# Fills that stay on one product before the level stage, four logarithms in one place, and an earlier split of the mLSTM read-out

## The reference, cut to what matters

```python
xn = _rms_norm(x, P['norm_mix_pre'][l])
cols = jnp.einsum('btd,dc->btc', xn, P['w_in'][l])
ca, cb, cc, cg = _split(cols, [A_COLS, B_COLS, C_COLS, N_BRANCH * D_MODEL])
h_a = mLSTM(ca)                 # mixer A, its read-out: sigmoid(o) * h
h_b = window_attention(cb)      # mixer B
h_c = rwkv(cc)                  # mixer C
gates = jax.nn.sigmoid(cg).reshape(Bsz, T, N_BRANCH, D_MODEL)
merged = (gates[:, :, 0] * (h_a @ P['w_branch_a'][l])
          + gates[:, :, 1] * (h_b @ P['w_branch_b'][l])
          + gates[:, :, 2] * (h_c @ P['w_branch_c'][l]))
mix = merged @ P['w_out'][l]
```

```python
mean = jnp.mean(y, axis=-1, keepdims=True)
var = jnp.mean(jnp.square(y - mean), axis=-1, keepdims=True)
y = ((y - mean) * lax.rsqrt(var + GN_EPS)).reshape(Bsz, T, C_W) * gn_g + gn_b
```

## Time and profile before

| | |
|---|---|
| median of 3 runs | 2463.97 us (2463.54 to 2465.94) |
| the profiled execution: its time, its span | 2466.26 us, 2464.5 us |
| PE busy | 2336.3 us, 95% |
| DVE, ACT, POOL busy | 997.6, 901.3, 786.4 us |
| ACT_TABLE_LOAD | 69 of 1283 ns |
| mean granted TensorE clock | 0.976 |

### The profile page before, as it was taken

How to read it: one execution, slowest core, us unless ns; L and a number is a source line. 1 busy time by engine, 2 the same in 40 slices (tenths; PEclk the granted TensorE clock), 3 DMA queues, 4 the chain that set the end, 5 groups by cost and what they waited for, 6 DMA issues and landing times.

```text
span 2464.5 us, 53615 instructions
## 1 busy us (share of the span) xinstructions
PE 2336.3 (95%) x23450; PEld 2225.3 (90%) x23450; DVE 997.6 (40%) x1559; ACT 901.3 (37%) x1751; POOL 786.4 (32%) x630
## 2 busy tenths in 40 slices
PE   7999989999899899999989999999998989999997
PEld 7998888888789899999989988888887989999997
DVE  4426654455434522320073276545444534332102
ACT  4345532213354522222344455223323444233222
POOL 3332222112235244444324222222112433444441
PEclk9999989999999999999999999999999999999998
DMA  5532211111214132322334221111112242233331
GB/s 162 135 88 65 61 36 32 28 49 32 60 50 143 57 91 86 90 86 86 82 107 130 61 74 48 28 49 32 28 41 63 72 131 61 87 92 89 89 86 52
DMA packets 334193, 180.82 MB, mean 73 GB/s; under 512 B 33528, under 2 KB 330648, under 8 KB 332936
## 3 DMA queue, kind: packets, MB, share of 16 engines
q1 hardware_dynamic: 333776, 177.34, 26.0%
q10 hardware_dynamic: 184, 0.05, 0.0%
HBM read 167.98 MB, written 9.38 MB: 72 GB/s over the span
## 4 chain that ended last, share of the span: by engine, by line
PE 81%; DVE 10%; ACT 4%; issue 3%; DMA 1%; POOL 1%; SPq 0%; DVEq 0%; ACTq 0%; POOLq 0%
PE psum_products L657 72%; PE psum_mixer L657 7%; DMA w_raw<-in_w_in 1%; ACT w_high L1221 1%; DVE xn_low L2047 1%; DVE merged L2041 1%; DVE x L1671 1%; ACT L1221 0%; ACT c_in_rate L1221 0%; DVE squares_ffn L1665 0%; DVE gate_product L2039 0%; POOL w_low L2270 0%; DVE squares L1638 0%; PE psum_mixer L1036 0%; SPq L2118 0%
## 5 line engine op out<-in xcount | busy, mean ns | idle before, releaser
L2270 POOL TENSOR_TENSOR w_low<-w_raw,w_high 128x512 fp32r<-128x512 f32 (+2 forms) x606 | 761.5, 1278 | 1562.4 <-ACT w_high L1221 1561.0
L657 PE MATMUL psum_products<-xn_high,w_high 128*128 128x272 f32 (+1 forms) x3424 | 741.3, 298 | 43.0 <-POOL w_low L2270 14.2
L657 PE MATMUL psum_products<-xn_high,w_low 128*128 128x272 f32 (+1 forms) x3424 | 713.2, 290 | 0.0
L657 PE MATMUL psum_products<-xn_low,w_high 128*128 128x272 f32 (+1 forms) x3424 | 712.1, 290 | 0.0
L657 PEld LDWEIGHTS psum_products<-xn_high,w_high 128*128 128x128 f32 x3424 | 545.1, 190 | 64.2 <-issue 32.8
L657 PEld LDWEIGHTS psum_products<-xn_low,w_high 128*128 128x128 f32 x3424 | 546.1, 191 | 0.0
L657 PEld LDWEIGHTS psum_products<-xn_high,w_low 128*128 128x128 f32 x3424 | 542.8, 191 | 0.0
L1221 ACT ACTIVATE w_high<-w_raw 128x512 fp32r<-128x512 f32 (+2 forms) x606 | 331.2, 595 | 169.8 <-PE psum_products L657 140.1
L657 PE MATMUL psum_products<-hidden_high,w_high 128*128 128x272 f32 x704 | 145.9, 288 | 0.0
L657 PE MATMUL psum_products<-hidden_high,w_low 128*128 128x272 f32 x704 | 145.7, 288 | 0.0
L657 PE MATMUL psum_products<-hidden_low,w_high 128*128 128x272 f32 x704 | 145.1, 288 | 0.0
(11 more groups left out here) (373 smaller groups left out, 2991.7 us busy)
## 6 DMA issues: line engine op xcount, KB each, us to landing
w_raw<-in_w_in SPq DMA_DIRECT2D x112, 512.0 KB, 4.0
w_raw<-in_w_ffn_in SPq DMA_DIRECT2D x88, 512.0 KB, 3.8
w_raw<-in_w_ffn_out SPq DMA_DIRECT2D x32, 512.0 KB, 3.9
w_raw<-in_w_out SPq DMA_DIRECT2D x16, 512.0 KB, 3.9
w_raw<-in_w_ffn_out SPq DMA_DIRECT2D x16, 384.0 KB, 3.3
x_kept<-x SPq DMA_DIRECT2D x2, 2176.0 KB, 7.6
x<-x_kept SPq DMA_DIRECT2D x2, 2176.0 KB, 9.0
w_raw<-in_w_in SPq DMA_DIRECT2D x16, 256.0 KB, 3.8
```

Of the source, the lines that this page charges most:

```text
L657: return pe.matmul(out, lhsT, rhs, start=start, stop=stop, skip_group_check=True)
L2270: low_ready.inc(pool.tensor_tensor(wl[:, n % NSPLIT, ks_], wraw[:, slot, ks_], wh[:, n % NSPLIT, ks_].bitcast(F32), ALU.subtract))
```

## The change

It has three parts. First, `fill` gets a second argument. In `c_prep`, `c_keys` and `c_scale` (which is `c_keys` on PE) it is False, and the fill then takes steps of the next unit alone. In the other steps it takes two units as before. Second, `c_variance` on ACT copies the variance out of PSUM (scale 1/64) instead of taking its logarithm, and `c_rsqrt` takes all logarithms (two instructions of 1090 columns) and then two Exps of the same size. DVE waits for the second Exp before block 2. Third, `a_out_split` moves from behind the last unit of `cols_c` to the place ahead of `b_out(8)`.

```diff
@@ WEIGHT @@
+          ... "a_out_split": 0.0 ...
@@ make_plan @@
             second += [("b_scores", l, c + 2)] if c < 7 else []
+            second += [("a_out_split", l)] if c == 7 else []
...
-        plan += [("a_out_split", l), ("gate", l) + GATES[0], ("c_shift_out", l)]
+        plan += [("gate", l) + GATES[0], ("c_shift_out", l)]
@@ tensor engine @@
-            def fill(steps):
+            def fill(steps, on=True):
...
-                while steps > 0 and u < len(units) and u < unit_at[0] + 2 and fillable(units[u]):
+                while steps > 0 and u < len(units) and u < unit_at[0] + 1 + on and fillable(units[u]):
...
-                fill(2)
+                fill(2, False)
...
-                fill(4)
+                fill(4, False)
...
             def c_keys(l, g):
-                fill(8)
+                fill(8, False)
@@ scalar engine @@
-                    step(fn(y_rn[:, f, c0:c1], mp[2 + b][:, 0:c1 - c0], ACT.Ln, scale=1.0 / 64, bias=C("scalars", 1, 1)),
-                         bank[2 + b].empty["act"])
+                    step(fn(y_rn[:, f, c0:c1], mp[2 + b][:, 0:c1 - c0], ACT.Copy, scale=1.0 / 64), bank[2 + b].empty["act"])
 
             def c_rsqrt(l):
-                step(fn(y_rn[:], y_rn[:], ACT.Exp, scale=-0.5), flow("c_gn_r"))
+                for f in (0, 2):
+                    step(fn(y_rn[:, f:f + 2, :], y_rn[:, f:f + 2, :], ACT.Ln, bias=C("scalars", 1, 1)))
+                for f in (0, 2):
+                    step(fn(y_rn[:, f:f + 2, :], y_rn[:, f:f + 2, :], ACT.Exp, scale=-0.5), flow("c_gn_r"))
@@ vector engine @@
-                if f == 0:
+                if f % 2 == 0:
                     flow("c_gn_r").wait_next(dve, "dve")
```

More of the change, by code:

```diff
@@ L165 @@
 WEIGHT = {"c_prep": 1.0, "c_keys": 1.0, "c_scaled": 0.3, "c_scale": 1.0, "c_gram": 0.7, "c_level": 0.3, "c_chain": 0.5,
-          "c_state_out": 0.0, "a_chunk": 0.6, "a_chunk_out": 0.5, "a_state_out": 0.0, "a_state_put": 0.0, "b_put": 0.0, "c_shift_put": 0.0, "c_state_put": 0.0, "a_scale": 0.3, "a_out": 0.2, "b_values": 0.5,
+          "c_state_out": 0.0, "a_chunk": 0.6, "a_chunk_out": 0.5, "a_out_split": 0.0, "a_state_out": 0.0, "a_state_put": 0.0, "b_put": 0.0, "c_shift_put": 0.0, "c_state_put": 0.0, "a_scale": 0.3, "a_out": 0.2, "b_values": 0.5,
           "b_scores": 0.6, "b_out": 0.6}
```

## The result

| | before | changed |
|---|---|---|
| median of 5 runs | 2463.54 us | 2450.94 us |
| lowest to highest | 2461.34 to 2465.94 | 2442.94 to 2457.63 |
| ratio, with its 95% interval | 1 | 0.9948 [0.9924, 0.9971] |
| profiled execution | 2466.26 us | 2442.94 us |

The change makes the kernel 12.6 us faster, where 18.6 us were forecast. The direction and the range hold, and so does the forecast's own range of 2439 to 2452 us, but the median lies 5.5 us above the predicted 2445.4 us. The changed kernel's runs spread over 14.7 us. A second set of runs in the experiments has a trace of a usual execution.

What follows compares the result with a forecast made beforehand. PE was taken to bound the kernel, busy 2336.3 of 2464.5 us. Per layer 5.9 + 3.4 + 0 = 9.3 us, 18.6 us for both, gave a median of 2445.4 us, range 2436 to 2460 us (forecast's own 2439 to 2452).

Steps and rivals of the forecast that it cites:

- The logarithms: Variance stage: 4.2 us of PE's idle time and 1.7 us of low clock won, 5.9 us per layer.
- The cover: Behind c_rsqrt: DVE's 2.59 us wait for PE and 3.0 us before branch C hide a 2.3 us later start.
- The fills: Groups of mixer C: ACT's and DVE's chain starts sooner, PE owes steps; 3.4 us per layer won.
- I leave that out: Steps PE owes go into levels, chains and variance, some filling a level that had none; this was not counted.
- the owed steps: Fill steps PE hasn't done by a group's first c_kprime product; in group 4 four steps, 2.9 us.
- The split: Read-out split at the attention's end: new 3.7 us wait against c_prep's clock; taken as 0, from -3.7 to +3 per layer.
- The prediction's sign against this term: The prediction is wrong in the read-out split if the clock stays at 0.5 in c_prep.
- A: Slower: PE waits for DVE in order at b_out and each c_scaled; 2471.6 us, chance 0.08.
- B: Only the squares' waits go, clock falls as often, fills win nothing; 8.4 us, 2455.6 us, chance 0.18.
- C: No change: PE's total work is the same and the waits only move; 2464 us, chance 0.08.
- D: More: POOL wait goes in full, clock stays high in c_prep and after; 16 us per layer, 2432 us, chance 0.08.

Runs made afterwards that it cites:

- logarithms alone: Kernel before, with only the variance blocks' logarithms gathered in c_rsqrt: 2451.23 us, ratio 0.9952.
- fills alone: Kernel before, with only the fills of c_prep, c_keys and c_scale kept on the next unit: 2451.39 us, ratio 0.9946.
- split alone: Kernel before, with only the read-out split moved ahead of b_out(8): 2467.74 us, ratio 1.0008.
- fills and logarithms: Kernel before, with the fill and logarithm edits together and the read-out split where it was: 2444.09 us, ratio 0.9917.
- changed, first trace: The whole change against the kernel before, first set of runs: median 2450.94 us, ratio 0.9948; its trace is the fastest execution, 2442.94 us.
- changed, once more: The whole change, unaltered, measured again against the kernel before: 2451.39 us, ratio 0.9945; trace of a usual execution, span 2451.0 us.
- split one step later: Changed kernel with the read-out split directly behind b_out(8), ahead of the last cols_c unit: 2436.88 us, ratio 0.9896 to the kernel before.
- c_prep only: Kernel before with the logarithm edit and only c_prep's fills kept on the next unit, split not moved: 2445.17 us, ratio 0.9921.

## Why the prediction was right or wrong

The stages of layer 0, each the difference of two starts in PE's timeline. The marks are the last probabilities' transposes, `c_tanh_w`'s product (mixer C begins), the first `c_kprime` product of groups 0 and 4, the first and the last squares' product, and branch C's first matmul:

```
                        transposes  mixer C   group 0   group 4    first      last        sum
                        -> mixer C  -> grp 0  -> grp 4  -> first   -> last    -> branch C
                                                        squares    squares
before                    16.86     22.07    296.69     33.96      26.07      32.54      428.19
logarithms alone          16.87     22.09    296.78     33.98      20.10      32.40      422.22
fills alone               16.85     22.08    290.34     33.83      25.63      32.52      421.25
split alone               21.32     18.97    298.26     33.99      24.49      32.53      429.56
fills and logarithms      16.85     22.09    290.61     33.80      22.68      32.40      418.43
changed, first trace      21.01     20.45    287.76     33.76      22.68      32.40      418.06
changed, once more        21.25     18.98    290.31     38.43      22.68      32.40      424.05
split one step later      15.27     21.44    291.91     33.81      22.68      32.40      417.51
```

The same in layer 1, of the kernels in which the layers differ, and of two to compare them with:

```
                        transposes  mixer C   group 0   group 4    first      last        sum
                        -> mixer C  -> grp 0  -> grp 4  -> first   -> last    -> branch C
                                                        squares    squares
before                    16.86     22.09    296.81     33.97      26.06      32.53      428.31
split alone               21.23     20.22    296.85     34.00      24.49      32.52      429.31
fills and logarithms      16.87     22.08    290.55     33.81      22.68      32.40      418.39
changed, first trace      19.90     21.66    288.94     33.83      22.68      32.40      419.40
changed, once more        19.90     21.41    289.18     33.83      22.68      32.40      419.40
split one step later      15.28     20.47    287.74     33.83      22.68      32.40      412.40
c_prep only               16.85     22.09    291.19     38.26      20.10      32.40      420.89
```

**The logarithms: right, and in size.** 26.07 - 20.10 = 5.97 us in the variance stage against the 5.9 of the forecast, and 11.8 us for both layers by the ratio. Of the 5.97 us some 1.7 us are clock, and that this part hangs on the wait, as the prediction says, isn't shown: the split alone kept the wait of 3.53 us and its stage ran at 1.00, 1.6 us shorter than before. The two loads and two logarithms in `c_rsqrt` were costed at nothing, and the column behind the last squares doesn't grow (32.54 to 32.40). PE has no wait for `c_out_low`. One size was low: the two Ln took 2.45 us where 2.0 were taken, and the two Exps 2.26 us where the one of 2180 columns took 2.02. I had scaled by columns and left out what each instruction costs by itself. The cover took it. The Trainium skill, "ScalarE: Activation LUTs", section "What ACT_TABLE_LOAD costs", puts some 0.28 us of an instruction with a bias operand down to the instruction itself, and 0.19 us to one without, which is near the 0.24 us that the second Exp added. The same section puts a switch of tables at about 2.66 us, of which 1.38 us is a drain. The trace doesn't bear that part out: the load took 1.28 us, the logarithm behind it began 0.01 us later (699.91 + 1.28 = 701.19, and 701.20), and the next load 0.02 us behind the logarithms (701.20 + 2.45 = 703.65, and 703.67).

**The fills: mechanism right, one term mis-sized.** The starts moved as worked out. From mixer C's start to group 1's first `c_kprime` it was 107.41 us before (434.23 - 326.82) and 98.56 us with the fills alone (423.21 - 324.65), so 8.85 us less (8.9 in the prediction). To group 4's it was 6.34 us less (22.07 + 296.69 against 22.08 + 290.34), and with the 2.9 us then owed that is 3.4 us, the forecast. In between it fits less well: the starts of groups 2 and 3 came 8.9 and 6.5 us earlier, where the working gives 7.3 and 4.4, so that the sum agrees at group 4 is in part luck. The step that failed is "I leave that out": I made PE pay those 2.9 us behind group 4. It didn't. From group 4 to the last squares this kernel took 59.46 us against 60.03, with the owed steps in it. They stand between the first and the last squares, where 1.9 us less idle time and 1.7 us less lost clock paid for them. So 6.9 us per layer were won, not 3.4. Where the logarithms had already taken the squares' wait and the low clock, the debt came due: the stage between the first and the last squares is 22.68 us with both, 20.10 with the logarithms alone. In that company the fills are worth 422.22 - 418.43 = 3.8 us per layer in the traces, against 3.4. For both layers that is 7.6 us, and 8.7 by the ratios or 7.1 by the medians, against 6.8. The wait for the gate's tanh, which the prediction didn't name in the sum, was inside the groups' starts.

**The split: the term that made the total wrong.** It stood at 0. It is 7 to 8 us of loss in company, and 2 us alone (with an interval that reaches to no loss), where the forecast's bounds were 3 us gained and 3.7 us lost per layer. The single pieces held: a wait of 3.05 us for the copy (3.7 worked out), `shift_out` gone, 1.63 us of `c_tanh_w` left (some 1.3), and `c_prep` 22.07 - 18.97 = 3.1 us quicker at full clock (3). By these pieces mixer C was to begin 3.7 - 1.75 = 1.95 us later, not the 2.1 of the text. What was missing is the clock between the new wait and mixer C. I let the wait cost its length and weighed its clock only as an alternative to the gain. In fact both came. The wait is followed by a clock of 0.75 over 11 us of solid work, 2.7 us, so mixer C begins 21.32 - 16.86 = 4.5 us later and not 2.1. 4.5 less 3.1 is a loss of 1.4 us in layer 0. In layer 1 it is 4.4 less 1.9, since `c_prep` ran at 0.69 there. From transposes to branch C the two layers lost 1.4 and 1.0 us, near the 2.0 us that the split alone measured, but that holds two more shifts of the clock: the variance stage 1.6 us shorter in each layer, and in layer 0 the groups 1.6 us longer. The prediction's sign against this term, a clock that stays at 0.5 in `c_prep`, came in layer 1 of the changed kernel (0.53) and not in layer 0 (0.69).

**What stays open.** A loss of 2 to 3 us alone isn't 7 to 8. In the second trace of the changed kernel the two layers are 6.6 us longer than with fills and logarithms (5.6 and 1.0), and 4.6 of it stand in one stage of layer 0 (38.43 against 33.80) where the order is the same in both and the clock was 0.66 for 15 us. In the first trace that stretch ran at 1.00, and the two layers are only 0.6 us longer (837.46 against 836.82). Over the whole span the two traces agree with this: 0.024 x 2451.0 = 58.8 us of lost clock against 0.021 x 2441.1 = 51.3 is 7.5 of the 9.9 us between them. So low clock makes the difference between these two traces. That it is what the moved split costs is not shown. The same low stretch stands in layer 1 of the kernel with `c_prep` only (38.26 us), which doesn't move the split, and the logarithms alone spread over 9.9 us. Each kernel has one or two traces, too few to tell how often a stretch falls low in which of them.

**The rivals.** A (DVE becomes the bound) is refuted for the fills, though the copy behind the subtractions is a wait of its kind: the product of group 2 kept its 0.69 us and that of group 3 its 1.09. The Trainium skill, "SBUF — State Buffer", section "Who interferes with whom", states that a DVE instruction with two SBUF inputs contends with a GpSimd instruction that reads SBUF. Group 1, which kept its 1.64 us beside POOL, is still in line with it, and so is group 4. But the change didn't carry the contention to other groups. B (only the squares' waits) is refuted by the fills alone. Its 2455.6 us is as near to the median (4.7 us off) as the forecast (5.5 us), but not for the reason that it gave: the clock did fall behind a new wait in the split. Behind the new waits for `c_kprime` it fell at times too (0.57 over 494 to 498 us in the first trace of the changed kernel, behind the wait of 2.35 us), but over all groups of that layer it was 0.98 as before. C fell with the logarithms: their interval ends at 0.9965. D had the fills about right in kind (7.1 per layer as upper end, 6.9 alone), but the wait for POOL didn't go in full (19.2 to 13.2).

## What to carry to other kernels

A new wait on the engine that sets the end is costed with the clock of the work behind it, even where it removes a low stretch further on: 3.05 us of waiting, with 1.4 us of other waits gone, cost 4.5 us here before anything was given back. Work that was pushed out of a chain was free here as long as idle time or a low clock waited behind it, and each gap can be filled once, so two edits that live off the same gap (here 9.5 us for the squares) must be summed over the gap and not over the edits. A stage that is compared in one layer is to be compared in the other too: the two layers of the last kernel differ by 5.1 us in one trace, more than some edits are worth. Where a moved step is to spare one engine a wait, try the place directly behind the instruction that others wait for. One step later turned the loss of 7 to 8 us into the lowest median of this study, though not clear of the kernel without the moved split.

## What the runs showed of the hardware

- The same instructions of the changed kernel ran at clock 1.00 in one execution and at 0.66 in another, over the 15 us ahead of the squares (33.76 against 38.43 us for the stage), with PE busy 92% and 96% of the time. The kernel with `c_prep` only shows the same between its two layers (34.00 and 38.26 us). No wait of PE in these stages is longer than 1.2 us. The figures are means between the two levels of 1.2 and 2.4 GHz.
- The mean clock of two executions, 0.979 and 0.976, went with 2441.1 and 2451.0 us. A difference of 0.003 in that column is worth more than some of the edits here. The five runs of the changed kernel that ranged over 14.7 us had 0.974 to 0.979, and the five that ranged over 2.8 us had 0.975 to 0.977.
- The wait of 3.05 us for the last probabilities stands in both layers of three traces (split alone, changed, changed once more). `c_prep` behind it ran at 1.00 in two of the six cases, in layer 0 of split alone and of changed once more, and at 0.53 to 0.69 in the other four.
- A wait of 3.53 us for the squares was followed by a low clock before (0.93 over the stage), and by 1.00 with the split alone.
- DVE's product of 128 columns with two operands in SBUF took 0.29 us when it began 0.12 us ahead of POOL's subtraction, and 1.36 to 1.38 us when it began 0.04 to 0.06 us behind it (before, fills and logarithms, changed once more). POOL's own time hardly changed (2.52 and 2.54 us for two).
